# A transformer stack on one core: the conditioning product moved from TensorE to GpSimd, in 32 pieces loaded beside the ring of weights

## The reference, cut to what matters

```python
mod = jax.nn.silu(c) @ w_ada[l] + b_ada[l]          # c: 1 x 1024, w_ada: 1024 x 6144
shift1, scale1, gate1, shift2, scale2, gate2 = jnp.split(mod[:, None, :], 6, axis=-1)
h = rms_norm_2(x, g_norm1[l]) * (1.0 + scale1) + shift1
...
x = x + gate1 * (merged @ w_out[l])
h2 = rms_norm_2(x, g_norm2[l]) * (1.0 + scale2) + shift2
...
x = x + gate2 * y_ffn
```

## Time and profile before

| | before |
|---|---|
| median of 3 executions | 1296.06 us (1295.61 to 1301.79) |
| profiled execution, its time | 1297.68 us |
| its span | 1295.8 us |
| TensorE busy | 1200.5 us (93% of the span) |
| VectorE busy | 840.3 us (65%) |
| ScalarE busy | 575.6 us (44%) |
| GpSimd busy | 99.7 us (8%) |
| mean granted clock | 0.971 |

### The profile page before, as it was taken

One profiled execution on the slowest core, in us unless ns is written; L12 is line 12 of the kernel. 1 busy time (PEld: TensorE's weight loads), 2 busy tenths in 40 slices (PEclk: granted clock), 3 DMA queues, 4 the chain that ended last, 5 costly groups with the idle time before them and its releaser, 6 DMA issues. The chain is left out here.

```text
span 1295.8 us, 18976 instructions
## 1 busy us (share of the span) xinstructions
PE 1200.5 (93%) x7132; PEld 946.6 (73%) x7132; DVE 840.3 (65%) x1587; ACT 575.6 (44%) x979; POOL 99.7 (8%) x131
## 2 busy tenths in 40 slices
PE   5998998999979997999879999989899999999997
PEld 4988776799767985789767768878566567666763
DVE  4656478566585648556456988676666666666664
ACT  4233365443564517343365334552154455544551
POOL 1040000510014000000010011000000000000000
PEclk9988798999989999999989999999899999999999
DMA  9453272465723644355513354212199999999980
GB/s 349 151 195 129 100 260 97 145 244 190 278 70 133 250 170 179 130 195 210 152 33 104 132 195 164 97 41 103 43 420 419 419 398 415 365 358 356 399 325 33
DMA packets 99402, 273.64 MB, mean 211 GB/s; under 512 B 14977, under 2 KB 20353, under 8 KB 83713
## 3 DMA queue, kind: packets, MB, share of 16 engines
q1 hardware_dynamic: 96160, 268.52, 55.6%
q10 hardware_dynamic: 3170, 4.14, 0.9%
HBM read 271.60 MB, written 1.05 MB: 210 GB/s over the span
## 5 line engine op out<-in xcount | busy, mean ns | idle before, releaser
L1507 ACT ACTIVATE weights_high<-ring 128x2048 fp32r<-128x2048 f32 (+2 forms) x88 | 160.4, 1866 | 194.9 <-PE psum L740 67.5
L1979 DVE TENSOR_TENSOR weights_low<-ring,weights_high 128x2048 fp32r<-128x2048 f32 (+2 forms) x88 | 194.4, 2242 | 30.4 <-ACT weights_high L1507 29.4
L740 PE MATMUL psum<-input_high,weights_high 128*128 128x256 f32 x480 | 138.3, 288 | 4.7 <-DVEq L2010 4.0
L740 PE MATMUL psum<-input_high,weights_low 128*128 128x256 f32 x480 | 137.7, 287 | 0.0
L740 PE MATMUL psum<-input_low,weights_high 128*128 128x256 f32 x480 | 137.5, 287 | 0.0
L2925 DVE TENSOR_TENSOR expert_low<-expert,expert_high 128x2048 fp32r<-128x2048 f32 x48 | 109.0, 2284 | 6.2 <-ACT expert_high L1777 6.2
L752 PE MATMUL psum<-weights_high,input_high 128*128 128x512 f32 (+2 forms) x272 | 102.7, 377 | 2.4 <-issue 1.9
L752 PE MATMUL psum<-weights_low,input_high 128*128 128x512 f32 (+2 forms) x272 | 101.4, 373 | 0.0
L752 PE MATMUL psum<-weights_high,input_low 128*128 128x512 f32 (+2 forms) x272 | 101.2, 372 | 0.0
L740 PEld LDWEIGHTS psum<-input_high,weights_high 128*128 128x128 f32 x480 | 94.1, 196 | 5.4 <-DVEq L2010 4.4
L1777 ACT ACTIVATE expert_high<-expert 128x2048 fp32r<-128x2048 f32 x48 | 91.2, 1913 | 12.5 <-DMA expert<-in_exp_gate_up 7.3
(11 more groups left out here) (412 smaller groups left out, 2589.6 us busy)
## 6 DMA issues: line engine op xcount, KB each, us to landing
expert<-in_exp_gate_up SPq DMA_DIRECT2D x80, 1024.0 KB, 9.2
expert<-in_exp_down SPq DMA_DIRECT2D x40, 1024.0 KB, 12.3
ring<-in_w_ada SPq DMA_DIRECT2D x12, 2048.0 KB, 8.5
ring<-in_b_w_in SPq DMA_DIRECT2D x8, 2048.0 KB, 9.1
ring<-in_d_w_in SPq DMA_DIRECT2D x8, 2048.0 KB, 9.1
ring<-in_a_w_in SPq DMA_DIRECT2D x7, 2048.0 KB, 9.0
ring<-in_c_w_in SPq DMA_DIRECT2D x7, 2048.0 KB, 7.9
ring<-in_w_in SPq DMA_DIRECT2D x7, 2048.0 KB, 7.8
```

Source lines behind the costliest of these rows:

```text
L740: last = nc.tensor.matmul(bank[:, 256 * f:256 * f + 256], w2_[x][:, d, col + 128 * f:col + 128 * f + 128], in2[y][:, d, :], start=(k == 0) ...
L1507: nc.scalar.activation(hi_half(m, k), ring[i][:, x], ACT.Copy).then_inc(s_wh, 1)
L1979: v.tensor_tensor(w_lo[i][:, x], ring[i][:, x], hi_half(m, k), ALU.subtract).then_inc(s_wl, 1)
```

## The change

GpSimd makes the product. The matrix comes in 32 pieces of 128 rows by 1536 columns (768 KB each, in the order of the four column groups, eight row groups in each) into a new tile `modulation_weights` with two halves, `ada[0]` and `ada[1]`. For a piece GpSimd multiplies the half in place by the column of `silu(c)` that belongs to its row group (one number per partition, `TENSOR_SCALAR` 128x1536) and adds it to `mod` (`TENSOR_TENSOR` 128x1536). `mod` then has 128 partial rows instead of four, and `pick` becomes all ones. Pieces 0 to 6 stand in layer A, 7 to 18 in B, 19 to 31 in C. SyncE issues a piece behind the ring load that `MOD_AFTER` names; from the third on it first waits until the piece before the previous one has been added (`s_pm`). TensorE's `modulation()`, VectorE's `mods` and the 12 ring loads go. `columns()` becomes 32 products of a 128x128 section with a single column of ones, into two banks, and VectorE copies 16 columns of each.

```diff
+ADA = 1536
-    a[:, CC["pick"][0]:CC["pick"][1]] = (p % 32 == 0)
+    a[:, CC["pick"][0]:CC["pick"][1]] = 1.0
+            ada_ = sb("modulation_weights", P, 2 * ADA, stack=early)
-        MOD = [cols(A["w_ada_2"][0], 512 * j, 512) for j in range(12)]
+        MOD = [(A["w_ada_2"][0][P * k:P * k + P, ADA * q:ADA * q + ADA], k, slice(ADA * q, ADA * q + ADA))
+               for q in range(6 * D // ADA) for k in range(DC)]
+        ada = [ada_[:, ADA * i:ADA * i + ADA] for i in range(2)]
+        MOD_AFTER = {11: 7, 16: 1, 17: 1, 18: 1, 19: 1, 20: 1, 21: 7, 25: 1, 26: 1, 27: 1, 28: 1, 29: 1, 30: 8}
...
                 done_at.append((s_oa, halves) if ahead is HALF else (acc_done, fills + ahead))
+                for _ in range(MOD_AFTER.get(n, 0)):
+                    if piece >= 2:
+                        sp.wait_ge(s_pm, piece - 1)
+                    sp.dma_start(ada[piece % 2], MOD[piece][0]).then_inc(s_ada[piece % 2], 16)
+                    piece += 1
                 n += 1
...
-            def modulation():
-
-                w = slot()[:, :].rearrange("p (c n) -> p c n", n=512)
-                a, _b = acc("d")
-                for d in range(DC):
-                    g = 32 * (d % 4)
-                    last = nc.tensor.matmul(a[g:g + 32, :], last_bc(siluc[:, d:d + 1], 32)[:, 0, :], w[:, d, :],
-                                            start=(d < 4), stop=(d >= 4))
-                last.then_inc(acc_done, 1)
...
             def columns():
+                pe.wait_ge(s_pm, len(MOD))
+                for base in ((0, D), (3 * D, 4 * D)):
+                    b = tr("td")
+                    for i in range(2):
+                        for d in range(DC):
+                            last = nc.tensor.matmul(b[:, 8 * i + d:8 * i + d + 1], mod[:, base[i] + 128 * d:base[i] + 128 * d + 128],
+                                                    ones_[:, 0:1], start=True, stop=True)
+                    last.then_inc(tr_done, 1)
...
+            def modulation(pieces):
+
+                for i in pieces:
+                    _src, k, x = MOD[i]
+                    pool.wait_ge(s_ada[i % 2], 16 * (i // 2 + 1))
+                    if i > 0:
+                        pool.wait_ge(s_pm, i)
+                    me.link(nc.gpsimd.tensor_scalar(ada[i % 2], ada[i % 2], siluc[:, k:k + 1], None, ALU.mult))
+                    nc.gpsimd.tensor_tensor(mod[:, x], ada[i % 2], mod[:, x], ALU.add).then_inc(s_pm, 1)
...
             nc.gpsimd.memset(mod[:, :], 0.0).then_inc(s_mz, 1)
+            pool.wait_ge(s_row, 16)
+            modulation(range(0, 7))
             tile_roots((0, 0, 1, 1))
             pool.wait_ge(s_attn, 1)
             alibi([x for x in slopes(8) for _ in range(2)], [0] * 16)
+            modulation(range(7, 19))
             for first, n, seen in ((0, 6, 12), (8, 6, 12), (6, 2, 14), (14, 2, 16)):
                 pool.wait_ge(s_sub, seen)
...
             alibi(slopes(12), [1 + i // 4 for i in range(12)])
+            modulation(range(19, 32))
             tile_roots((0, 0, 1, 1))
...
-                    if n in mods_after:
-                        mods(1)
```

More of the change, by code:

```diff
@@ L270, in build @@
         s_mz = sem("mod_zeroed")
+        s_ada, s_pm = [sem(f"modulation_weights_in{i}") for i in range(2)], sem("modulation_pieces_added")
         s_scaled, s_fin = sem("experts_scaled"), [sem(f"final_ready{t}") for t in range(T)]
@@ L471, in build, with later_units @@
         HALF = None
-        def with_mods(units, after, mods, early=2):
-            blocks = iter(MOD[mods:mods + len(after)])
-            stream = []
-            for n in range(units):
-                if early <= n + 1 < units:
-                    stream.append((None, 1, 0))
-                if n in after:
-                    stream.append((next(blocks), 1, 0))
-            return stream
+        def later_units(units, early=2):
+            return [(None, 1, 0)] * (units - early)
         OUTS = []
@@ L868, in head_values, with attention @@
                 last.then_inc(o_done, 1)
-            def attention(units, blocks, dv, last_block, more_at, mods_after=()):
+            def attention(units, blocks, dv, last_block, more_at):
                 nk0 = 128 if blocks is CAUSAL else 256
@@ L2078, in o_in, with attention @@
                 return free["o", i], c.up(("o", i))
-            def attention(units, blocks, put, over, last_block, mods_after=(), after=None, between=None):
+            def attention(units, blocks, put, over, last_block, after=None, between=None):
                 nb = 128 * len(blocks)
```

53 lines of the change are left out of this document (16 added, 37 removed).

## The result

| | before | after |
|---|---|---|
| median of 4 executions | 1295.84 us (1293.84 to 1301.79) | 1401.38 us (1400.53 to 1407.35) |
| ratio to before, 95% interval | | 1.0819 [1.0794, 1.0844] |
| span of the profiled execution | 1295.8 us | 1399.6 us |
| mean granted clock | 0.971 | 0.929 |

What follows compares the result with a forecast made beforehand. TensorE, busy 93%, was taken as the bound, with GpSimd's roots delaying everything behind them; +2 (A), +38 (B), +46 (C), +4 (clock), +3 (columns()) gave +93 us on 1297.7, against the median 1389 us; range 1330 to 1420.

Steps and rivals of the forecast that it cites:

- What bounds the kernel: Whole kernel: TensorE busy 93%; GpSimd's 8% hides three small root instructions on the way of everything behind them.
- One piece, 7.9 us: GpSimd, both 128x1536 instructions: 4.2 us one-input by a straight line, 3.5 two-input, with semaphores 7.9 us (5.2 to 8.6).
- The rival with the memset's rate: GpSimd's one-input form is fast in long instructions: piece 5.2 us, +47, total 1343 us; chance 0.25.
- Layer A, +2: Layer A: 10.5 us of products removed, 12 us of VectorE waits for GpSimd added; +2 us (-2 to +14).
- 0.9 us (0.2/0.85 of 4.2): Layer A: how long GpSimd's one-input instruction of 4.2 us holds VectorE's two-operand form out, scaled from one of 850 ns.
- Layer B, +38: B's head roots, due at 364.26, wait behind seven pieces until 402: +38 us (+19 to +43).
- layer C, +46: C's first root, due at 520.92, waits behind eight pieces until 567: +46 us (+23 to +52).
- The projections, 0 (to +10): Pieces 7 to 11 and 19 to 23 beside projections cost 0 (to +10), VectorE's halves having time in hand.
- The third rival: VectorE-GpSimd waits reach ten blocks in B and C, 2 us each, layer A at upper end: 1421 us; chance 0.08.
- Clock, +4: TensorE works at the lower clock for some us after each of the two pauses: +4 us.
- columns(), +3: The new columns(), 32 one-column products at 0.12 us a record, takes 7.7 us against 4.6: +3 (0 to +7).
- The rival on the other side: GpSimd finishes before B's and C's roots need it, products simply gone: -15, total 1281 us; chance 0.03.

Runs made afterwards that it cites:

- experiment 7: Changed kernel with no piece loaded, multiplied or added, new columns() kept: 1330.48 us, 1.0260 to before, with one additional experts' round of about 42 us.
- experiment 1: Changed kernel without the 15 pieces behind the last input blocks of B and C: 1358.69 us, 1.0481 to before, with one additional experts' round.
- experiment 9: Changed kernel with the full product spread: nine pieces in A, seven in B, eight in C, eight in D, columns() four projections later: 1357.80 us, 1.0492 to before.
- experiment 6: Changed kernel without the five pieces beside B's projections and their loads: 1431.62 us, 1.1038 to before; A's root to B's last input block 107.0 us.
- experiments 4 and 5: Changed kernel with one of each piece's two GpSimd instructions left out: multiply only 1372.71 us, 1.0586 to before; add only 1368.13 us, 1.0551.
- experiments 3, 7 and 8: Changed kernel with transposes in columns(), product whole: 1397.63 us; without pieces, new columns(): 1330.48 us; without pieces, old columns() by transposes: 1324.75 us.
- experiment 3: Changed kernel with columns() back to transposes and VectorE's sums, product whole: 1397.63 us, 1.0790 to before.

## Why the prediction was right, and where it was not

**What bounds the kernel, and where most of the loss arises**: right. TensorE had no room and GpSimd's 8% hid three small instructions that everything behind them waits for. The loads came in time: in B GpSimd works from 358.49 to 414.32 without a wait for a transfer.

**One piece, 7.9 us**: 7.85 measured. The straight line from 16 and 256 columns held at 1536 (4.16 us for 4.2), and so did the two-input form (3.44 for 3.5). The rival with the memset's rate falls here. The Trainium skill, "GPSIMD Engine Reference", § 4.1 Engine selection, calls one-input operations "roughly line-rate"; the row doesn't agree: 4158 ns for 1536 columns is 2.7 ns a column, three times the memset's 0.85.

**Layer A, +2**: +3.7, and that the sum came so near is luck, since two sizes were too small. The gain was 12.65 us and not 10.5, mostly in the first unit with a product: it took 8.5 us before (148.82 to 157.31, at the lower clock) and 3.6 in experiment 7, so 4.9 went and not 3.0. The loss was 16.4 us and not 12. It was to lie in the scalings of 13 units. In fact 8.4 us lie there, and 8.0 behind the last unit, which the prediction had not looked at: a half of 128x2048 took 4.77 us instead of 2.28, the scaling behind it 2.71, and TensorE waited. TensorE in time order:

```profile
206.40 2.83 PE L857 MATMUL psum<-V,probsT 128*128 128x64 f32 x12 [5.27 <-DVE u L2430]
```

From 201 to 216 the granted clock was 0.50. Within the units the mis-sized step is the hold of the one-input form, "0.9 us (0.2/0.85 of 4.2)". It was taken as a share of the instruction, where the rows of after show 3.15 us, so that the last 1.0 us of it is free (and 0.65 of the one of 850 ns). With 3.15 and 3.2 in each 7.85 us the same formula gives a mean wait of 1.28 us, and the scalings of the units in step waited 1.17 in the mean. That agreement should not be leaned on: the formula takes the phase to be random, and the units ran in step with the pieces.

**Layer B, +38, and layer C, +46**: +35.4 and +46.3, and experiment 1 gives 84.4 back. That these agree to 3 us in B rests on the count of pieces and the length of one, and on the place of the first, which the ring load ahead of it sets: 358.49 measured, 10.9 after B's last input block, where the prediction had 10. The end predicted for B was 402 (404 on the changed clock). It came at 414.3, since B's own projections had become longer. In C the same count holds, 84.3 us from the block to the root where the prediction had 84. But experiment 9 loses 14.0 of the 46 in C's attention with GpSimd idle for 22 us before the root, so pieces at that place cost something in any order; of the 46 the order alone is at most about 32.

**The projections, 0 (to +10)**: this is the step that failed, in B: +10.9, experiment 6. "VectorE's halves have some us in hand" was right of a block in which VectorE has nothing else to do, 5.0 us, and C's pairs of 8.3 to 9.2 us instead of 4.5 cost it nothing (from the root in B's tail, 388.98 before and 438.06 after, to C's last input block it takes 93.9 us before and 94.1 after). What was left out is VectorE's other work on two SBUF operands in the same blocks. B has two such instructions that C has not, L2494 and L2497, and they took 8.8 us instead of 2.6; together with the 3.9 us of the pair before them that is more than there was in hand. The halves of the next two blocks then waited for GpSimd as well, 10.4 and 10.9 us a pair, with TensorE behind them. That these two instructions make the difference between B and C is read from the traces; no kernel without them was run. Half a piece held only one of them, and cost nothing (experiments 4 and 5). The third rival named the mechanism, with 2 us in every one of ten blocks; it was 11 us, all in B.

**Clock, +4, and columns(), +3**: together with the opening of D +9.3 measured. The 0.12 us a record came from records with 64 columns; those with one column take 0.16. So `columns()` took 10.1 us for 4.3, +5.8, and 1.7 us of lower clock stand behind it, not only behind the pauses. The 5.3 to 5.5 us of experiments 3, 7 and 8 are the same with the clock in them, against transposes, which took 6.0 in experiment 3. The opening of D came out 1.8 us longer.

**The rival on the other side**, GpSimd done in time: its condition, a piece of 2.6 us, was far off. In B half a piece misses it already (experiments 4 and 5). Where GpSimd was done in time, in C with the addition alone, the gain did not come, because of the exclusion.

The sum was 93 and the change cost 105.5, 105.1 by the last root: the projections of B make 11 of the 12 us, and the other differences (+1.7 in A, -2.6 in B's attention, +2.3 in D) nearly cancel.

## What to carry to other kernels

Before work is given to an engine that looks idle, list the small instructions on it that others wait for, and count the queue up to each of them: on an engine that was 8% busy, pieces in front of two roots cost this kernel 84 us (experiment 1). Price long GpSimd instructions also by what VectorE does with two SBUF operands beside them; even a 128x4 instruction then waits, and moving the pieces to another place moves the waits with them. Count all of VectorE's two-operand work in a block against the time in hand, not only the instruction that the next engine waits for. A straight line from two short instructions of the same form predicted an instruction's time well, but not the part of it that excludes another engine.

## What was not expected of the hardware

- VectorE's form with two SBUF operands was let in 3.15 us after the start of a GpSimd one-input instruction of 4.16 us, and after 3.2 to 3.3 of 3.44 us of a two-input one. The exclusion works both ways: GpSimd's two-input instruction took 4.56 us when VectorE was inside, and 128x1536 in the one-input form up to 8.13.
- Its size is that of GpSimd's instruction and not of VectorE's: a 128x4 instruction of 0.16 us took 1.34 in the median and 2.71 at most, one of 128x384 3.5 to 3.7 instead of 0.56.
- Products of one column in plain float32 with a 128x128 section as weights took 0.16 us a record, two records each, and TensorE worked at the lower clock for 4 us behind them, which it did not behind 128-column transposes in the same place. After a pause of 8 us all 64 records ran at the lower clock (experiment 9).
